# A two-block network on one core: the first head's four slabs projected from raw instead of normalised tokens

## The chip, the cores and the metric

The kernel runs on one core of one Trainium2 chip. The metric is the device time of one execution in microseconds. The kernel before takes 1519.56 us, the median of three runs (1519.48 to 1520.62). A profiled execution, from which every row below comes, is one execution with the hardware profiler on.

The engines are named as the profile names them: PE is TensorE (matmuls), PEld its weight loads, DVE is VectorE, ACT is ScalarE, POOL is GpSimd, and SP is SyncE, which here only issues DMAs.

## The reference

Two blocks over 512 tokens with 1024 features, all in float32. What matters here is how the first block begins: the tokens are normalised, and one wide projection feeds everything else.

```python
def rmsnorm(x, g):
    xf = x.astype(jnp.float32)
    y = xf * lax.rsqrt(jnp.mean(xf * xf, axis=-1, keepdims=True) + EPS)
    return (y * g.astype(jnp.float32)).astype(x.dtype)

h = rmsnorm(x, norm1_g[l])
(hg_q, hg_f, hg_i, hg_g, ml_qk, ml_v, ml_if, ml_o,
 mb_z, mb_xbc, mb_dt, gate_pre) = jnp.split(h @ w_in[l], split_at, axis=-1)
log_f = jnp.log(lb + (1.0 - lb) * jax.nn.sigmoid(hg_f.astype(f32)))
o_hg = hgrn2_scan(jax.nn.silu(hg_q)..., log_f..., hg_i...)     # 8 heads, 128 wide
y_hg = rmsnorm(o_hg, hg_norm_g[l]).reshape(B, S, HG_W) * jax.nn.silu(hg_g)
```

The normalisation is a product per token and a gain per feature: h[t, d] = x[t, d] * g[d] * r[t], with r[t] the reciprocal root mean square of token t. Since r does not depend on d, (h @ W)[t, :] = r[t] * ((x * g) @ W)[t, :]. After the projection come three recurrent branches (HGRN2, mLSTM and Mamba-2), their gated mix, a feed-forward network, and a second block with convolution and windowed attention.

## The kernel before, in words

**Tiles.** Features lie on the 128 partitions and tokens along the free dimension, so a normalised activation is eight feature tiles of 128x512. Weights come as slabs: 128 output columns by 1024 inputs, 512 KB each, 245 of them, through four slots of the tile `raw` in the order in which they are used. Float32 accuracy is reached by splitting each operand in a high half, rounded to the type that PE takes at full pace, and a low half, the rest: `wh` and `wl` of a weight slab (ScalarE rounds `wh`, GpSimd subtracts for `wl`, in two halves at L447), `hh` and `hl` of the normalised tokens, `yh` and `yl` of other activations. `project` issues, for each of the eight feature tiles, three matmuls of 128x512: high times high (L519), high weight times low data (L522), low weight times high data (L523), all into one PSUM bank.

**Order of the work.** Each engine has a program written out by hand, with semaphores between them. PE's program is a row of projections with the branches' small matmuls put between them: the slabs of head u+1 are projected while head u's recurrence is evaluated. Head 0 therefore has only its four slabs F, Q, G, I (numbers 0 to 3) in the prologue, and slab 4 is the first that is projected inside the head loop (`hg_tile(0, ...)`).

**The prologue.** The token rows arrive in four blocks of 128 (`xs`). ScalarE squares and sums each, and makes r for two blocks at a time (L1061, L1065, L1067). DVE multiplies (`xn`, L1708). PE turns the blocks by transposes into six PSUM banks (L549; the last two tiles later, L562), ScalarE reads a bank with the gain into `hh` (L1074), DVE the rest into `hl` (L1715). PE then projects slab 0 tile by tile as the halves appear, with slab 1 interleaved, and slabs 2 and 3. The high halves of slabs 0 to 3 are made by ScalarE, DVE and twice by GpSimd. Two bias matmuls (L555) go in between. Behind the projections, ScalarE and DVE turn head 0's results into its gate and its query (`hg_sigmoid`, `hg_forget`, `hg_first`, L1752 to L1763), and DVE rounds the matrices `onr` and `kbr` (L1771, L1773), for which PE waits before the head loop. Head 0's first sums are L1904 to L1911 on DVE.

**Banks.** Projections alternate between the two banks `acc[0]` and `acc[1]`, which `acc_free0` and `acc_free1` hand back; the others, `b2` to `b7`, belong to the branches.

Of the kernel before, what the change touches and what calls it, by code (L numbers as in the profile page):

```python
# [93 lines left out]
W_LINE = 1024  # L94

# [38 lines left out]
def build(nc, slabs, x, xt, par_d, const_d, onehot_d, bias_scratch, row_scratch, out):  # L134
    with ExitStack() as ctx:
        start = -(-nc.sbuf_base // 64) * 64

        def arena(at):
# [57 lines left out]
        names = """params_in ident_in onr_set masks_in x_in0 x_in1 x_in2 x_in3 onehot_in pre_hi slab_hi slab_split slab_used acc_free0 acc_free1 zero_set  # L196
            pre_h1 xt_in pro_sq pro_rs pro_n pro_tr nrm_rs nrm_h nrm_hi nrm_lo lt_sq lt_add lt_hi lt_lo lt_ss lt_step lb_step
# [9 lines left out]
            at_silu at_sq at_sl kbr_set at_ss at_tr at_rs at_v at_n at_nh at_nl at_s at_l at_mx at_ex at_sum at_p at_pt at_o at_y  # L207
# [198 lines left out]
        def _(sp):  # L406
# [7 lines left out]
            for b in range(NB):  # L414
                sp.dma_start(xs[:, b, :], x.rearrange("a (b p) d -> p (a b) d", p=P)[:, b, :]
                             ).then_inc(S[f"x_in{b}"], 16)
            for j in range(4):
                load(j, j, 0)
                if j == 1:
                    sp.dma_start(oneh[0:64, :], onehot_d[0:64, :]).then_inc(S["onehot_in"], 16)  # L420
# [15 lines left out]
        def _(pool):  # L436
            nc.gpsimd.memset(zero[:, :], 0.0).then_inc(S["zero_set"], 1)
            pool.wait_ge(S["zero_set"], 1)
# [11 lines left out]
            pool.wait_ge(S["pro_n"], NB)  # L450
            pool.wait_ge(S["pre_hi"], 1)
            slab_lo(0)
            pool.wait_ge(S["pre_h1"], 1)
            slab_lo(1)
            for j in (2, 3):
                pool.wait_ge(slab_in[j], 16)
                pool.tensor_tensor(slab(wh, j), slab(raw, j), zero[:, 0:1].broadcast_to([P, KT * P]), ALU.add
                                   ).then_inc(S["pre_hi"], 1)
                pool.wait_ge(S["pre_hi"], j)
                slab_lo(j)  # L460
            def slabs_lo(first, end):
                with pool.Fori(first // 4, end // 4) as it:
                    for i in range(4):
                        pool.wait_ge(S["slab_hi"], it * 4 + (i - 3))
                        slab_lo(i)
# [9 lines left out]
            pool.wait_ge(S["slab_hi"], J_SMALL - 3)  # L475
# [20 lines left out]
            slabs_lo(J_MB0 + 7, N_SLABS)
            for j in range(N_SLABS // 4 * 4, N_SLABS):
                pool.wait_ge(S["slab_hi"], j - 3)
# [4 lines left out]
        def _(pe):  # L503
            mm = pe.matmul

            def project(j0, it=None, k=0, src=(hh, hl), n=KT, base=0, t0=None, first=True, last=True,
                        ready=(), order=(), lo=None, late=None):

                t0 = j0 if t0 is None else t0
                bank, s = acc[t0 % 2], j0 % 4  # L510
                pe.wait_ge(S["slab_split"], lin(2 * (j0 + 1), it, 2 * k) if lo is None else lo)
                if first:
# [31 lines left out]

            pe.wait_ge(S["ident_in"], 16)
            for b in range(NB):
                pe.wait_ge(S["pro_n"], b + 1)
                for f in range(6):
                    ins = pe.transpose(blk(psum[2 + f], b), xn[:, b, f * P:(f + 1) * P], ident)  # L549
                    if b == NB - 1:  # L550
                        ins.then_inc(S["pro_tr"], 1)
            pe.wait_ge(S["params_in"], 16)
            pe.wait_ge(S["onehot_in"], 16)
            for c in range(2):
                mm(acc[1][32 * c:32 * c + AT_HEADS, :], par[0:64, PAR["rel"]:PAR["rel"] + AT_HEADS],  # L555
                   oneh[0:64, c * T:(c + 1) * T], start=True, stop=True).then_inc(S["wb_mm"], 1)

            def turn_in(f):

                pe.wait_ge(S["nrm_lo"], f - 5)  # L560
                for b in range(NB):
                    ins = pe.transpose(blk(psum[2 + f % 6], b), xn[:, b, f * P:(f + 1) * P], ident)  # L562
                ins.then_inc(S["pro_tr"], 1)

            def first(f):

                project(J_HG, order=(f,), first=f == 0, last=f == KT - 1, ready=[(S["nrm_hi"], f + 1)],
                        late=(S["nrm_lo"], f + 1), lo=1 if f < KT // 2 else 2)

            def second(f):  # L570

                project(J_HG + 1, order=(f,), first=f == 0, last=f == KT - 1, lo=3 if f < KT // 2 else 4)
# [55 lines left out]
            def hg_half(s, u, p, j0, it):  # L628
                U = unit[p]
                before = not isinstance(u, int) or u > 0  # L630
                if s == 2:
                    pe.wait_ge(S["hg_ph"], u + 1)
# [405 lines left out]
        def _(act):  # L1038
# [19 lines left out]
            def norm_in():  # L1058
                for b in range(NB):
                    act.wait_ge(S[f"x_in{b}"], 16)  # L1060
                    A(xq[:, b, :], xs[:, b, :], ACT.Square, accum_out=x_ss[:, 0, b:b + 1]).then_inc(S["pro_sq"], 1)  # L1061
                    if b % 2:
                        ss, rs = x_ss[:, 0, b - 1:b + 1], x_ss[:, 1, b - 1:b + 1]
                        act.wait_ge(S["pro_sq"], b + 1)
                        A(rs, ss, ACT.Ln, scale=1.0 / D, bias=EPS).then_inc(S["pro_rs"], 1)  # L1065
                        act.wait_ge(S["pro_rs"], b)
                        A(rs, rs, ACT.Exp, scale=-0.5).then_inc(S["pro_rs"], 1)  # L1067
                act.wait_ge(slab_in[0], 16)
                A(wh[:, 0].rearrange("p k f -> p (k f)"), raw[:, 0].rearrange("p k f -> p (k f)"), ACT.Copy
                  ).then_inc(S["pre_hi"], 1)  # L1070
                act.wait_ge(S["params_in"], 16)
                for f in range(KT):
                    act.wait_ge(S["pro_tr"], f + 1)
                    A(hh[:, f, :], psum[2 + f % 6][:, :], ACT.Identity, scale=pc("norm1", f)  # L1074
                      ).then_inc(S["nrm_hi"], 1)
                    if f == 2:
                        act.wait_ge(S["wb_mm"], 2)
                        for c in range(2):
                            A(wrow[:, c * T:(c + 1) * T], acc[1][32 * c:32 * c + AT_HEADS, :], ACT.Copy
                              ).then_inc(S["wb_ev"], 1)  # L1080
                    if f == 3:
                        act.dma_start(con[:, K_BD:N_CONST], const_d[:, K_BD:]).then_inc(S["masks_in"], 16)
# [1576 lines left out]
```

## Time and profile before

| | us |
|---|---|
| median of three runs | 1519.56 |
| the profiled execution's own time | 1519.61 |
| its span, first to last instruction | 1517.8 |
| PE busy | 1504.9 |
| VectorE busy | 809.9 |
| ScalarE busy | 737.8 |
| GpSimd busy | 665.3 |

The span is what the profile's rows cover; the execution's own time is 1.8 us longer. Times in the rows are counted from the span's start. A matmul of 128x512 is shown with 0.39 us, but one starts every 0.227 us, since they are pipelined: durations of PE overlap, and starts are what counts. The granted clock is the share of full speed that the chip's throttle is recorded to have allowed PE.

### The profile page before, as it was taken

Reading aid. Unit: us, or ns where it says so; the run is one execution under the profiler, and the core shown is the slowest. Engines: PE = TensorE matmul, PEld = TensorE weight load, DVE = VectorE, ACT = ScalarE, POOL = GpSimd, SP = SyncE. Lnnn points to the kernel's source line nnn. Section 1 sums busy time; section 2 is a strip of 40 time slices with the busy share of each in tenths; the row PEclk is TensorE's granted clock in tenths of the full one; section 3 lists DMA queues with packets and bytes.
Section 4 is the critical chain, followed back from the end, with each engine's and each line's share of the span. In section 5 each row is a group of like instructions: output and inputs, shape, how many; then the busy total and the mean of one; then the engine's idle time right before and its main releaser. Section 6 shows DMA issues by size and latency. Waiting matters only on the chain.

```text
span 1517.8 us, 20835 instructions
## 1 busy us (share of the span) xinstructions
PE 1504.9 (99%) x7144; PEld 1231.6 (81%) x7144; DVE 809.9 (53%) x1387; ACT 737.8 (49%) x1177; POOL 665.3 (44%) x510
## 2 busy tenths in 40 slices
PE   7999999999999999999999999999999999999999
PEld 6888888888888888888888888888888887777777
DVE  4677778542347731677633445554542335756761
ACT  6667665424346432466653444444443344545551
POOL 5433433444544454343344444444455554334432
PEclk9999999999999999999999999999999999999999
DMA  5222222333322333223333323333333342222222
GB/s 191 84 70 70 83 70 70 97 97 114 125 84 70 107 116 97 83 100 109 105 110 96 95 96 97 96 97 97 97 99 109 110 140 91 84 94 94 84 58 95
DMA packets 40023, 147.21 MB, mean 97 GB/s; under 512 B 4400, under 2 KB 4912, under 8 KB 38928
## 3 DMA queue, kind: packets, MB, share of 16 engines
q1 hardware_dynamic: 37088, 132.79, 27.4%
q10 hardware_dynamic: 2864, 13.45, 2.3%
q8 instruction: 47, 0.77, 0.2%
q14 instruction: 24, 0.20, 0.0%
HBM read 144.05 MB, written 2.18 MB: 96 GB/s over the span
## 4 chain that ended last, share of the span: by engine, by line
PE 98%; DVE 1%; ACT 0%; DMA 0%; issue 0%; SPq 0%; DVEq 0%
PE bank L519 27%; PE bank L523 27%; PE bank L522 27%; PE bank L736 3%; PE bank L1008 3%; PE bank L623 1%; PE bank L754 1%; PE bank L927 1%; PE bank L917 1%; PE bank L908 1%; PE bank L676 0%; PE bank L999 0%; PE bank L678 0%; DMA xs<-x 0%; PE bank L664 0%; PE bank L549 0%
## 5 line engine op out<-in xcount | busy, mean ns | idle before, releaser
L447 POOL TENSOR_TENSOR wl<-raw,wh 128x512 fp32r<-128x512 f32 x488 | 645.6, 1345 | 831.5 <-ACT wh L1051 819.8
L519 PE MATMUL bank<-hh,wh 128*128 128x512 f32 x832 | 331.6, 399 | 0.1
L523 PE MATMUL bank<-hh,wl 128*128 128x512 f32 x832 | 324.6, 390 | 0.0
L522 PE MATMUL bank<-hl,wh 128*128 128x512 f32 x832 | 324.0, 389 | 0.0
L1051 ACT ACTIVATE wh<-raw 128x1024 fp32r<-128x1024 f32 x241 | 252.8, 1051 | 134.3 <-DMA raw<-slabs 134.2
L519 PE MATMUL bank<-yh,wh 128*128 128x512 f32 x800 | 314.7, 393 | 0.6 <-DVE au L2354 0.4
L523 PE MATMUL bank<-yh,wl 128*128 128x512 f32 x800 | 311.5, 389 | 0.0
L522 PE MATMUL bank<-yl,wh 128*128 128x512 f32 x800 | 311.5, 389 | 0.0
L523 PEld LDWEIGHTS bank<-hh,wl 128*128 128x128 f32 x832 | 156.1, 188 | 33.7
L519 PEld LDWEIGHTS bank<-hh,wh 128*128 128x128 f32 x832 | 156.3, 188 | 33.1 <-issue 2.7
L522 PEld LDWEIGHTS bank<-hl,wh 128*128 128x128 f32 x832 | 156.5, 188 | 30.9
L519 PEld LDWEIGHTS bank<-yh,wh 128*128 128x128 f32 x800 | 150.2, 188 | 36.9 <-issue 6.5
L523 PEld LDWEIGHTS bank<-yh,wl 128*128 128x128 f32 x800 | 150.2, 188 | 31.8
L522 PEld LDWEIGHTS bank<-yl,wh 128*128 128x128 f32 x800 | 150.2, 188 | 30.2
L2297 DVE TENSOR_TENSOR f_t<-bank,rsn 128x512 f32<-128x512 f32 x44 | 30.4, 692 | 110.8 <-PE bank L523 108.4
L519 PE MATMUL bank<-fh,wh 128*128 128x512 f32 x176 | 68.5, 389 | 0.0
L522 PE MATMUL bank<-fl,wh 128*128 128x512 f32 x176 | 68.5, 389 | 0.0
L523 PE MATMUL bank<-fh,wl 128*128 128x512 f32 x176 | 68.5, 389 | 0.0
L2260 DVE TENSOR_TENSOR xT<-xT,bank 128x512 f32<-128x512 f32 x16 | 11.0, 688 | 101.0 <-PE bank L523 101.0
L1863 DVE SCALAR_TENSOR_TENSOR unit<-bank,par,unit 128x511 f32<-128x511 f32 (+2 forms) x72 | 53.9, 749 | 2.6
L1565 ACT ACTIVATE f_g<-f_t,par 128x512 f32<-128x512 f32 x22 | 18.0, 816 | 67.5 <-DVE f_t L2297 67.4
L1686 ACT ACTIVATE a_l<-a_l,a_st 128x512 f32<-128x512 f32 x32 | 23.2, 724 | 45.5 <-DVE a_st L2399 45.4
(356 smaller groups left out, 2021.0 us busy)
## 6 DMA issues: line engine op xcount, KB each, us to landing
raw<-slabs SPq DMA_DIRECT2D x245, 512.0 KB, 3.5
xT<-row_scratch ACTq DMA_DIRECT2D x6, 1024.0 KB, 4.8
xs<-x SPq DMA_DIRECT2D x4, 512.0 KB, 5.8
xT<-xt ACTq DMA_DIRECT2D x2, 1024.0 KB, 7.0
wb<-bias_scratch ACTq DMA_DIRECT2D x1, 1792.0 KB, 8.7
wb<-bias_scratch ACTq DMA_DIRECT2D x2, 896.0 KB, 4.4
out<-a_l SPq DMA_DIRECT2D x4, 256.0 KB, 4.7
out<-au SPq DMA_DIRECT2D x3, 256.0 KB, 2.0
```

The costliest lines, as they stand in the source:

```text
L447: pool.tensor_tensor(slab(wl, i, half), slab(raw, i, half), slab(wh, i, half).bitcast(F32), ALU.subtract).then_inc(S["slab_split"], 1)
L519: mm(bank[:, :], wh[:, s, b, :], xh, start=first and i == 0, stop=False)
L522: mm(bank[:, :], wh[:, s, b, :], xl, start=False, stop=False)
L523: ins = mm(bank[:, :], wl[:, s, b, :], xh, start=False, stop=last and i == len(order) - 1)
L623: ins = mm(dims((b3, b2)[j % 2], a * P // 2, (P, 2), (1, P // 2)), blk(zk[j % 3], a), dims(zq[j % 4], P * a + h, (2 * P - h, 2), (2 * h, n ...
L736: ins = mm(bank[:, :], blk(x_[:, k, :], b), w[u][:, n * T:(n + 1) * T], start=k == 0 and c == 0, stop=k == KT - 1 and c == 2)
L1008: ins = mm(bank[:, :], w[u][:, n * T + b * P:n * T + (b + 1) * P], v[:, k, :], start=i == 0 and n == 0 and c == 0, stop=i == 3 and n == 1 ...
L1051: A(wh[:, i].rearrange("p k f -> p (k f)"), raw[:, i].rearrange("p k f -> p (k f)"), ACT.Copy).then_inc(S["slab_hi"], 1)
L1565: A((f_g, f_v)[v][p][:, :], f_t[v][:, :], ACT.Identity, scale=pc("fcw", lin(3 * NF * v + 3 * p + 2, it, 6)), bias=pc("fcb", lin(p + NF * v ...
L1686: A(a_l[i % 4][:, :], a_l[i % 4][:, :], ACT.Exp, bias=a_st[:, i, 0:1], accum_out=a_st[:, i, 1:2]).then_inc(S["at_ex"], 1)
L1863: ins = STT(dst[:, s:], bank[:, 0:T - s], pc(w, 4 * i + k), dst[:, s:], ALU.mult, ALU.add)
L2297: TT(f_t[v][:, :], acc[j0 % 2][:, :], rsn[:, :], ALU.mult).then_inc(acc_free[j0 % 2], 1)
```

## The change

Slabs 0 to 3 are no longer projected from normalised tokens. SP now loads the transposed raw tokens (`xT`, in three parts) right behind slab 0. ScalarE multiplies by the gain and rounds into `yh`, DVE makes the rest `yl`, and PE projects F, Q, G and I from these, with F and Q in `acc[0]` and `acc[1]`, G in `b6` and I in `b7`. Before them stand 12 matmuls on a zeroed tile. ScalarE makes the high halves of all four slabs.

The token rows are still loaded, behind slabs 1 and 2, for their sums of squares. The factors r are laid on the diagonals of four 128x128 blocks (`rs_diag`) and multiplied by a matrix of ones, which spreads them over all partitions of `b2`; ScalarE copies them to `rs_all`. `raw_out` multiplies each of the four results by `rs_all`. For all later slabs, DVE makes the normalised tiles from `xT`, gain and `b2` in two PSUM banks in turn (`normed`), ScalarE rounds them to `hh` (`normed_hi`), and DVE subtracts for `hl` (`normed_lo`). PE's slab 4 waits for them.

```diff
+            load(0, 0, 0)
+            for i in range(3):
+                features_in(i)
+            load(1, 1, 0)
+            tokens_in(0)
+            load(2, 2, 0)
+            tokens_in(1)
+            load(3, 3, 0)
...
+            pe.wait_ge(S["zero_set"], 2)
+            for _ in range(WARM):
+                mm(blk(b5, 0), spare[:, :], spare[:, :], start=True, stop=True)
+
+            for f in range(KT):
+                project(J_HG + HG_F, src=(yh, yl), order=(f,), first=f == 0, last=f == KT - 1,
+                        ready=[(S["raw_hi"], f + 1)], late=(S["raw_lo"], f + 1), lo=1 if f < KT // 2 else 2)
+            project(J_HG + HG_Q, src=(yh, yl))
+            project(J_HG + HG_G, src=(yh, yl), order=range(2), last=False, own=b6)
             pe.wait_ge(S["ident_in"], 16)
             for b in range(NB):
...
+                pe.wait_ge(S["pro_d"], b + 1)
+                ins = mm(blk(b2, b), ones, rs_diag[:, b, :], start=True, stop=True)
+            ins.then_inc(S["pro_b"], 1)
+            project(J_HG + HG_G, src=(yh, yl), order=range(2, KT), first=False, own=b6)
+            project(J_HG + HG_I, src=(yh, yl), own=b7)
...
-            first(0)
-            first(1)
-            turn_in(6)
-            first(2)
-            turn_in(7)
-            pe.wait_ge(S["wb_ev"], 2)
-            for f in range(3, KT):
-                second(f - 3)
-                first(f)
-            for f in range(KT - 3, KT):
-                second(f)
-            for i in range(2, 4):
-                project(J_HG + i)
             pe.wait_ge(S["masks_in"], 16)
-            pe.wait_ge(S["onr_set"], 1)
-            pe.wait_ge(S["kbr_set"], 1)
+            pe.wait_ge(S["ones_set"], 2)
...
-                    project(j, it, 8)
+                    project(j, it, 8, ready=[(S["nrm_lo"], f + 1) for f in range(KT)] if it is None and u == 0 else ())
...
+            def raw_out(i, bank, done):
+
+                dve.wait_ge(S["slab_used"], i + 1)
+                if i == HG_G:
+                    TT(unit[0][:, i, :], bank[:, :], rs_all[:, :], ALU.mult).then_inc(done, 1)
+                    return
+                (a, b), (p, q), (c, d) = even_odd(bank[:, :]), even_odd(rs_all[:, :]), slots(unit[0][:, i, :])
+                TT(c, a, p, ALU.mult)
+                TT(d, b, q, ALU.mult).then_inc(done, 1)
+
+            def normed(f):
+
+                wait(dve, S["nrm_lo"], f - 1)
+                STT((b3, b4)[f % 2][:, :], xT[:, f, :], pc("norm1", f), b2[:, :], ALU.mult, ALU.mult).then_inc(S["nrm_t"], 1)
+
+            def normed_lo(f):
+
+                dve.wait_ge(S["nrm_hi"], f + 1)
+                TT(hl[:, f, :], (b3, b4)[f % 2][:, :], hh[:, f, :].bitcast(F32), ALU.subtract).then_inc(S["nrm_lo"], 1)
```

On ScalarE, this is the start of the program before, from the table load to the first high halves (`xq` squares, `x_ss` factors):

```order
L1045 ACT_TABLE_LOAD
L1061 ACTIVATE xq,x_ss<-xs 128x1024 [waits x_in0]
L1061 ACTIVATE xq,x_ss<-xs 128x1024 [waits x_in1]
L1065 ACTIVATE x_ss<-x_ss 128x2 [waits pro_sq]
L1067 ACTIVATE x_ss<-x_ss 128x2 [waits pro_rs]
...
L1069 ACTIVATE wh<-raw 128x1024 [waits slab_in0]
L1074 ACTIVATE hh<-bank,par 128x512 [waits pro_tr,params_in]
```

And the same place now, where `wh<-raw` is a slab's high half and `yh<-xT` a raw feature tile's:

```order
L1047 ACTIVATE wh<-raw 128x1024 [waits slab_in0]
L1072 ACTIVATE yh<-xT,par 128x512 [waits f_in0,params_in]
L1072 ACTIVATE yh<-xT,par 128x512 [waits f_in0]
L1072 ACTIVATE yh<-xT,par 128x512 [waits f_in1] x2
L1072 ACTIVATE yh<-xT,par 128x512 [waits f_in2] x4
L1047 ACTIVATE wh<-raw 128x1024 [waits slab_in1]
L1075 ACTIVATE small<-small 128x8 [waits lb_step]
L1053 ACTIVATE xq,x_ss<-xs 128x1024 [waits x_in0] x2
```

The squares moved behind the eight feature tiles and slab 1's high half; slab 1's high half, before on DVE, stands behind all eight feature tiles.

On DVE, this is the end of the prologue before, from head 0's gate to its first sum:

```order
L1752 TENSOR_SCALAR hg_88<-hg_86,small 128x512 [waits hg_f,lb_step]
L1761 TENSOR_SCALAR hg_90<-hg_88 128x512 [waits hg_k]
L1763 TENSOR_TENSOR hgq_95<-unit_62,hg_88 128x512 [waits hg_silu]
L1768 COPY hga_93<-pair 128x512
L1768 COPY hga_94<-pair 128x512
L1771 CAST onr<-con 128x128 [waits ident_in,lb_step]
L1773 CAST kbr<-con 128x128 [waits masks_in]
L1774 TENSOR_TENSOR small<-par 128x8
L1904 TENSOR_TENSOR hgp<-unit_62,hg_90 128x512 [waits hg_z]
```

And now its last part (L1786 is `normed`, L1791 `normed_lo`, L1780 and L1781 `raw_out` of I):

```order
L1786 SCALAR_TENSOR_TENSOR bank<-xT,par,bank 128x512 [waits nrm_lo]
L1791 TENSOR_TENSOR hl<-bank,hh 128x512 [waits nrm_hi]
L1769 TENSOR_SCALAR hg_91<-hg_89 128x512 [waits hg_k]
L1771 TENSOR_TENSOR hgq_96<-unit_62,hg_89 128x512 [waits hg_silu]
L1786 SCALAR_TENSOR_TENSOR bank<-xT,par,bank 128x512 [waits nrm_lo]
L1791 TENSOR_TENSOR hl<-bank,hh 128x512 [waits nrm_hi] x2
L1780 TENSOR_TENSOR unit_62<-bank,rs_all 128x256 [waits slab_used]
L1781 TENSOR_TENSOR unit_62<-bank,rs_all 128x256
L1820 CAST kbr<-con 128x128 [waits masks_in]
L1821 TENSOR_TENSOR small<-par 128x8
L1951 TENSOR_TENSOR hgp<-unit_62,hg_91 128x512 [waits hg_z]
```

Sixteen instructions on the normalised tiles now stand between the copied factors and `kbr`, in between head 0's own.

On PE, the step into slab 4 before:

```order
L519 MATMUL bank<-hh,wh 128x512
L522 MATMUL bank<-hl,wh 128x512
L523 MATMUL bank<-hh,wl 128x512
L519 MATMUL bank<-hh,wh 128x512 [waits slab_split,kbr_set,acc_free0,onr_set,masks_in]
L522 MATMUL bank<-hl,wh 128x512
```

And now, after slab I and the two bias matmuls (`oneh`):

```order
L529 MATMUL bank<-yh,wl 128x512
L570 MATMUL bank<-oneh,par 8x512 [waits onehot_in,params_in]
L570 MATMUL bank<-oneh,par 8x512
L525 MATMUL bank<-hh,wh 128x512 [waits acc_free0,slab_split,nrm_lo,ones_set,masks_in]
L528 MATMUL bank<-hl,wh 128x512
L529 MATMUL bank<-hh,wl 128x512
L525 MATMUL bank<-hh,wh 128x512 [waits nrm_lo]
```

The bias matmuls moved here, and each tile of slab 4 waits for its low half; `ones_set` reaches 2 with `kbr`.

## Rows read from the trace of the kernel before

**Rows 1.** The page: span and busy time of two engines.
```profile
span 1517.8 us, 20835 instructions
...
PE 1504.9 (99%) x7144; PEld 1231.6 (81%) x7144; DVE 809.9 (53%) x1387; ACT 737.8 (49%) x1177; POOL 665.3 (44%) x510
```

**Rows 2.** Waits of PE, whole span: total us, times, longest.
```profile
PE bank L549 <- DVE xn L1708: 9.1, 1, 9.1
PE bank L917 <- DVE a_l L2407: 0.6, 2, 0.3
```

**Rows 3.** Chain of waits, in order of time: start us, us, what.
```profile
1.19 5.36 DMA xs<-x
...
9.12 5.14 PE bank L549 x24
14.26 0.96 PE bank L555 x4
```

**Rows 4.** Timeline of PE: start us, us, engine, line, operation.
```profile
37.96 0.39 PE L519 MATMUL bank<-hh,wh 128*128 128x512 f32 x1
...
43.40 0.62 PE L623 MATMUL bank<-hgq,hgk 128*128 128x128 f32 x4
```

**Rows 5.** Stretches: busy us of each engine, granted clock, DMA share, GB/s.
```profile
0.00:9.80 9.80, 0.68 (x4) 0.71 (x5) 1.42 (x2) 5.60 (x10) 0.30 (x5) 1.00 0.81 308
...
37.95:1517.80 1479.85, 1476.07 (x7013) 1207.81 (x7011) 792.20 (x1356) 713.69 (x1138) 644.72 (x491) 1.00 0.29 95
```

**Rows 6.** Timeline of ACT in the prologue.
```profile
4.71 1.06 ACT L1061 ACTIVATE xq<-xs 128x1024 f32<-128x1024 f32 x1 [1.75 <-DMA xs<-x]
...
17.11 2.43 ACT L1074 ACTIVATE hh<-bank,par 128x512 fp32r<-128x512 f32 x4
...
30.07 1.28 ACT L1042 ACT_TABLE_LOAD   x1
```

**Rows 7.** Timeline of POOL in the prologue.
```profile
19.64 2.54 POOL L447 TENSOR_TENSOR wl<-raw,wh 128x512 fp32r<-128x512 f32 x2
...
30.13 2.54 POOL L447 TENSOR_TENSOR wl<-raw,wh 128x512 fp32r<-128x512 f32 x2 [3.48 <-ACT wh L1051]
34.34 6.08 POOL L447 TENSOR_TENSOR wl<-raw,wh 128x512 fp32r<-128x512 f32 x4 [1.67 <-ACT wh L1051]
```

**Rows 8.** Timeline of DVE in the prologue.
```profile
17.24 3.38 DVE L1715 SCALAR_TENSOR_TENSOR hl<-bank,par,hh 128x512 fp32r<-128x512 f32 x5 [0.86 <-ACT hh L1074]
...
25.31 0.42 DVE L1723 TENSOR_SCALAR unit<-bank 128x256 f32<-128x256 f32 x1 [4.35 <-PE bank L523]
25.65 0.41 DVE L1724 TENSOR_SCALAR unit<-bank 128x256 f32<-128x256 f32 x1
...
28.17 0.55 DVE L1752 TENSOR_SCALAR hg<-hg,small 128x512 f32<-128x512 f32 x1 [1.09 <-ACT hg L1169]
28.75 0.43 DVE L1761 TENSOR_SCALAR hg<-hg 128x512 f32<-128x512 f32 x1
32.03 1.19 DVE L1763 TENSOR_TENSOR hgq<-unit,hg 128x512 f32<-128x512 f32 x1 [2.85 <-ACT unit L1153]
...
33.92 0.23 DVE L1771 CAST onr<-con 128x128 fp32r<-128x128 f32 x1
...
34.28 0.68 DVE L1904 TENSOR_TENSOR hgp<-unit,hg 128x512 f32<-128x512 f32 x1
34.88 1.51 DVE L1905 TENSOR_TENSOR hgp<-hgq,hg 128x256 f32<-128x256 f32 x1
...
41.72 0.95 DVE L1911 TENSOR_TENSOR hgpl<-hgp,hgph 128x768 fp32r<-128x768 f32 x1
```

**Rows 9.** Instructions that touch the tile con: duration ns min/median/max, starts, forms.
```profile
L549 PEld LDWEIGHTS bank<-con,xn x24: 178/230/230, 9.1 to 13.8; 128*128 128x128 f32 x24
...
L562 PEld LDWEIGHTS bank<-con,xn x8: 138/140/143, 16.4 to 18.0; 128*128 128x128 f32 x8
```

More of the change, by code:

```diff
@@ L94 @@
 W_LINE = 1024
+WARM = 12
 def ml_slab(u, i):
@@ L448, in slab_lo @@
                                        ).then_inc(S["slab_split"], 1)
[L450 to L459, printed above, removed]
+            for j in range(4):
+                pool.wait_ge(S["slab_hi"], j + 1)
                 slab_lo(j)
@@ L506, in project @@
             def project(j0, it=None, k=0, src=(hh, hl), n=KT, base=0, t0=None, first=True, last=True,
-                        ready=(), order=(), lo=None, late=None):
+                        ready=(), order=(), lo=None, late=None, own=None):
                 t0 = j0 if t0 is None else t0
-                bank, s = acc[t0 % 2], j0 % 4
+                bank, s = acc[t0 % 2] if own is None else own, j0 % 4
                 pe.wait_ge(S["slab_split"], lin(2 * (j0 + 1), it, 2 * k) if lo is None else lo)
-                if first:
+                if first and own is None:
                     wait(pe, acc_free[t0 % 2], lin(t0 // 2, it, k // 2))
@@ L554, in _ @@
             for c in range(2):
[L555 removed]
+                mm(b5[32 * c:32 * c + AT_HEADS, :], par[0:64, PAR["rel"]:PAR["rel"] + AT_HEADS],
                    oneh[0:64, c * T:(c + 1) * T], start=True, stop=True).then_inc(S["wb_mm"], 1)
[L558 to L572, printed above, removed]
[L574 to L586 removed]
             pe.wait_ge(S["masks_in"], 16)
[L588 to L589 removed]
+            pe.wait_ge(S["ones_set"], 2)
             def sum_all(bank, h, l, sem):
@@ L1056, in _, with first_hi @@
             exp_tables()
[L1058 to L1070, printed above, removed]
+            def first_hi(j):
+                act.wait_ge(slab_in[j], 16)
+                A(wh[:, j].rearrange("p k f -> p (k f)"), raw[:, j].rearrange("p k f -> p (k f)"), ACT.Copy
+                  ).then_inc(S["slab_hi"], 1)
@@ L1076, in norm_in @@
[L1076 to L1082, printed above, removed]
-                        act.wait_ge(S["wb_ev"], 2)
-                        act.dma_start(bias_scratch, wrow[:, :]).then_inc(S["wb_out"], 16)
+                    act.wait_ge(S[f"f_in{min(f // 2, 2)}"], 16)
@@ L1735, in _, with clamp_f @@
             dve.wait_ge(S["lb_step"], 6)
+            dve.wait_ge(S["ident_in"], 16)
+            dve.tensor_copy(onr[:, :], ones).then_inc(S["ones_set"], 1)
+            for b in range(NB):
+                dve.wait_ge(S["pro_rs"], b // 2 * 4 + 4)
+                TS(rs_diag[:, b, :], ident, x_ss[:, 1, b:b + 1], None, ALU.mult).then_inc(S["pro_d"], 1)
+            for i in range(2):
+                dve.tensor_copy(at2[i][:, :], zero[:, 0:1].broadcast_to([P, T])).then_inc(S["lb_step"], 1)
+            def clamp_f(j0, dst, it=None):
+                dve.wait_ge(S["slab_used"], lin(j0 + 1, it, 8))
+                (a, b), (c, d) = even_odd(acc[j0 % 2][:, :]), slots(dst)
+                TS(c, a, -40.0, None, ALU.max)
+                TS(d, b, -40.0, None, ALU.max).then_inc(acc_free[j0 % 2], 1)
             step = [0]
```

146 lines of the change are left out of this document (92 added, 54 removed).

## The prediction

> **What bounds the kernel now.** I read the page first. TensorE (PE) is busy for 1504.9 of 1517.8 us, VectorE (DVE), the next, for about half [rows 1]. PE's waits come next: 9.1 us in one piece at the start, and the next largest group is 0.6 us in two [rows 2]. So the program is a wait of 9.1 us, a prologue, and then a dense stream of matmuls. The chain of waits shows what the 9.1 us are: the token rows' DMA (and, between its rows, ScalarE's squares), then PE's transposes [rows 3]. The timeline of PE gives the boundary I work with: the first matmul of slab 4 (the first slab of head 1) issues at 37.96 us, the next block's first at 43.40 [rows 4]. A slab is therefore 5.44 us: 24 matmuls at 0.227, or 0.68 per feature tile. What follows 37.96 has 1476 busy us in 1480 [rows 5] and is not touched. The change is worth the shift of that boundary, called S, plus any stall that it leaves behind. The profiled execution took 1519.61 us, 1.8 more than its span and 0.05 above the median of the three timed runs (1519.56); I add the shift to 1519.61.
>
> **The change: what PE could gain.** Removed from PE are the 24 + 8 transposes and the wait for the normalised tokens. Added are 12 matmuls on zeros, four small matmuls of the factors and a wait before slab 4. The new front end needs slab 0, the constants and parameters, the feature tiles and slab 1, in SP's new order. At the rate of before, 308 GB/s over the first 9.8 us, 3.02 MB are in by then [rows 5]. Slab 0, constants and parameters are 0.92 MB and all features 2.10 more, so the last features land at 9.8, with 0.3 us to the semaphore 10.1; slab 1 (3.54 MB) follows at 11.8 at the latest.
> ScalarE starts slab 0's high half when it has landed, at 4.7 like the first token block [rows 6], and it lasts 1.0 to 1.06; POOL's two halves take 2.54 [rows 7], so they end at 7.1 and 8.4. DVE's first low feature tile has two inputs in SBUF and, I take it, waits behind POOL until 8.4, done at 9.1. The other seven follow at 0.68, so the F slab ends at about 14.4. Then PE stands: ScalarE makes slab 1's high half only after its eighth feature tile. Four tiles at 0.60 (four took 2.43 [rows 6]) after 10.1 is 12.5; the copy of slab 1 ends at 13.5; POOL's 2.54 ends at 16.05, with the semaphores 16.2. Slab Q starts at 16.2.
> From there PE issues Q (5.44), two tiles of G (1.36), four factor matmuls (eight records, 0.75; four such take 0.62 with their tail [rows 4]), the rest of G (4.08) and I (5.44), and the bias matmuls (0.96 [rows 3]). It would be ready for slab 4 at 34.2 us, 3.7 earlier than before. The zero matmuls end by about 6 us, before any operand is there, and cost nothing.
>
> **The new wait.** Slab 4 now needs all of hh and hl, and the rounded mask block (kbr), which is the last of DVE's new list. All of that list starts after the factors are spread over a bank and copied: 16.2 + 5.44 + 1.36 + 0.75 + 0.2 for the tail + 0.6 for ScalarE's copy + 0.1 = 24.65 us. From there DVE issues, all in a row:
> eight products xT*gain*factor at 0.67 = 5.36 (five of the same form took 3.38, that is 0.67 from one start to the next [rows 8]); eight subtractions at 0.60 = 4.80 (a TENSOR_TENSOR of 128x512 starts at 34.28, the next instruction at 34.88 [rows 8]); six half-bank products for F, Q and I at 0.34 = 2.04 (25.31 to 25.65), and G 0.60; clamp 0.42, forget 0.55, kk 0.33, zq 0.60, kbr 0.23 [rows 8]. The sum is 14.93, to 39.6.
> Three things lengthen it. The last subtraction needs ScalarE's eighth copy, which stands behind silu(G) and a table load of 1.28 [rows 6]; walking both lists by these durations ScalarE is 0.9 late there. Four products wait for the subtraction issued just before them instead of overlapping it, 0.3 in all. The product zq meets POOL's slab 5: the same instruction took 1.19 at 32.03 with POOL in its slab, and a like one 0.68 at 34.28 before POOL began [rows 7, 8], so 0.5. Slab 4 starts at 41.3 instead of 37.96: +3.35 us. PE idles from 34.2 to 41.3, 7.1 us.
> Bounds: without contention and with the first 0.3 saved, 39.6 (+1.6); with each of the 16 long instructions a full 0.74, half of those beside POOL's two slabs held to 1.5, and slab Q at 16.7, about 44 (+6). I take 3.35 because every term is the nearest row.
> How much DVE suffers from POOL is where a rule of the Trainium skill can be weighed. The rows: beside POOL's 34.34 to 40.42, the instruction of 256 columns with two SBUF inputs at 34.88 took 1.51, while the five with a PSUM input at 17.24, the last two of them beside POOL's 19.64, kept 0.67 [rows 7, 8]. The Trainium skill, SBUF — State Buffer, section "Who interferes with whom", says that a VectorE instruction with two SBUF inputs blocks against GpSimd and one with at most one does not; by that rule, which the trace agrees with, the 16 new instructions, each with a PSUM input, are free of it. Were the trace otherwise, and each such instruction 0.85 longer, as the 34.88 row is against the 0.67, the five or six that lie beside slabs 4 and 5 would add some 4 us, and S would be 45.
>
> **The clock.** The granted clock column shows 1.00 in every stretch [rows 5], but the instructions tell otherwise. After 9.1 idle us 24 transposes take 5.14 us, 0.214 each [rows 3], and their weight loads 230 ns in the median; eight later ones of the same shape load in 140 ns [rows 9]. I read that as the lower of the two levels (1.2 GHz) from 9.1 to about 13.8, 4.7 us, and 2.4 GHz after. After 7.1 idle us I expect the same: 4.7 us of slab 4 at half the clock, in which half the work is done, a loss of 2.35. Bounds: 0 (the fall does not come) and 4.7; by the pace of the transposes alone (0.214 against 0.14) it would be 1.6.
> The Trainium skill, TensorE: Matmul & The Clock Gate, section "What's actually happening", likewise has an idle array at 1.2 GHz by default and back at 2.4 after sustained work, which speaks against a change that opens a gap in a dense stream.
>
> **Who comes late afterwards.** Head 0's remaining sums need DVE from the first gate product (34.28) to hgpl's end (42.67), 8.4 us; PE asks for them about 8.55 us after S (slab 4's 5.44, two small products, four tiles of slab 5 at 0.68) [rows 8]. Now DVE starts them at S, so 0.15 us remain, and POOL has two halves there instead of four. ScalarE is about as late. I charge 0; if it shows, 1 us.
>
> **Sum.** +3.35 + 2.35 = +5.7: 1525.3 us.
>
> **Rivals.**
> B, the same wait, no clock fall. For it: the granted clock row never leaves 1.00 [rows 5]. Against: the slow transposes. 1519.6 + 3.35 = 1523.0.
> C, faster: DVE keeps up, PE alone sets the prologue and slab 4 starts at 34.2, -3.7: 1515.9. It decides when DVE's list after 24.65 takes 9.5 us or less. For it: two-input work is the costly part, and single-input instructions of 512 columns take 0.43 (28.75 [rows 8]); if all 16 took that, the list would still be 11.7. Against: every 512-column row with two inputs is at 0.67 or above.
> D, slower still: the front gap is felt too. After the zero matmuls end near 6 us, PE has one matmul until 9.1; if the F slab then runs wholly at the half pace (24 at 0.43 = 10.3) it ends at 19.4, Q starts 3.2 later, and everything behind with it: 1528.5. If the pace recovers in 4.7 us as before, only 0.6.
> E, the change does what it says but the features come later than the old rate allows: part of D in effect.
>
> **Chances.** Forecast 0.60, B 0.22, C 0.05, D with E 0.13. About 0.2% (3.0 us) is what a measurement of this kernel can tell from no change, so "same" is 1516.5 to 1522.6: it takes somewhat under half of B, whose spread of 1.5 us reaches there, and a little of C. Faster 0.04, same 0.11, slower 0.85. The range 1521.6 to 1529.0 takes in B, most of the forecast's bounds, and D.
>
> **What would show it.** Right: PE idle before slab 4's first matmul for 5 to 9 us, released by DVE (kbr or the last subtraction); a PE idle of 1 to 3 us between F and Q, released by POOL; slab 4's weight loads slow at its start; the body unchanged. Wrong: slab 4 starting before 38 us (C); no slow matmuls behind the gap (B); F's matmuls 0.43 apart (D); PE waits beyond 45 us, which I hold to be nothing.

## Result, and the profile after

| | before | after |
|---|---|---|
| time, median (lowest to highest; runs) | 1519.89 us (1519.48 to 1520.62; 5) | 1526.43 us (1525.80 to 1526.58; 5) |
| profiled execution: time, span | 1519.61, 1517.8 | 1526.43, 1524.0 |

The five runs of before are the three of the forecast and two more. The ratio is 1.0041, with a 95% interval of 1.003 to 1.0052: slower by more than the 0.2% that can be told. The forecast was 1525.3 us, the range 1521.6 to 1529.0. In the table and in every comparison below a single execution is only read for its profile; times are medians.

The page of after, against [rows 1]: PE is busy 5.3 us more with as many instructions as before, so some of them take longer.
```profile
span 1524.0 us, 20912 instructions
...
PE 1510.2 (99%) x7144; PEld 1234.9 (81%) x7144; DVE 824.3 (54%) x1408; ACT 743.5 (49%) x1184; POOL 659.3 (43%) x509
```
PE's waits, against [rows 2] (total us, times, longest). The 9.1 us at the start have become several short ones, and one of 6.3 us that the mask block kbr, the last of DVE's list, ends. It was to be 7.1.
```profile
PE bank L525 <- DVE kbr L1820: 6.3, 1, 6.3
PE bank L525 <- ACT yh L1072: 1.5, 1, 1.5
PE bank L553 <- POOL spare_row L452: 1.0, 1, 1.0
PE bank L528 <- DVE yl L1719: 0.8, 1, 0.8
...
PE bank L525 <- POOL wl L461: 0.3, 1, 0.3
```
PE's timeline, against [rows 4]. The F slab starts at 7.78, Q at 16.48, slab 4 at 41.25 (before: 37.96), and the block behind it at 49.39 (before: 43.40). Slab 4 therefore takes 8.14 us and not 5.44. Behind its first matmul (0.77) the line at 41.81 is the first of eleven that take 0.63 and start 0.43 apart; from 46.87 they start about 0.23 apart. Head 0's first sums come at 52.61.
```profile
7.78 0.47 PE L525 MATMUL bank<-yh,wh 128*128 128x512 f32 x1 [1.53 <-ACT yh L1072]
...
16.48 0.50 PE L525 MATMUL bank<-yh,wh 128*128 128x512 f32 x1 [0.30 <-POOL wl L461]
...
33.93 1.03 PE L570 MATMUL bank<-oneh,par 64*8 64x512 f32 x4
41.25 0.77 PE L525 MATMUL bank<-hh,wh 128*128 128x512 f32 x1 [6.29 <-DVE kbr L1820]
41.81 0.63 PE L528 MATMUL bank<-hl,wh 128*128 128x512 f32 x1
...
49.39 0.62 PE L607 MATMUL bank<-hgq,hgk 128*128 128x128 f32 x4
...
52.61 0.39 PE L622 MATMUL bank<-hgph,onr 128*128 128x512 f32 x1
```
Stretches of after (columns as in [rows 5]). The granted clock is about half (0.53) for nine matmuls of F and again (0.50) in the first part of slab 4, and full in between.
```profile
9.04:12.48 3.44, 3.44 (x9) 2.66 (x9) 3.36 (x6) 2.61 (x5) 0.00 (x0) 0.53 1.00 410
...
16.48:34.90 18.42, 18.42 (x84) 14.43 (x84) 11.64 (x26) 12.69 (x22) 7.32 (x6) 1.00 0.55 189
...
41.25:46.51 5.26, 5.26 (x13) 4.10 (x14) 5.13 (x8) 4.63 (x9) 3.79 (x3) 0.50 0.05 9
...
49.39:1524.00 1474.61, 1470.77 (x6989) 1203.37 (x6987) 790.63 (x1350) 709.23 (x1129) 637.42 (x487) 1.00 0.30 95
```
The same last stretch of before:
```profile
43.40:1517.80 1474.40, 1470.62 (x6989) 1203.31 (x6987) 787.61 (x1350) 709.82 (x1129) 641.64 (x489) 1.00 0.29 95
```
So the span's 6.2 us are 3.29 (41.25 less 37.96), 2.70 (8.14 less 5.44) and 0.21 (1474.61 less 1474.40).

DVE's timeline of after, against [rows 8]: the first product, the product zq, the last subtraction, kbr, one of head 0's instructions of 256 columns, and the rounding remainder hgpl.
```profile
25.13 0.76 DVE L1786 SCALAR_TENSOR_TENSOR bank<-xT,par,bank 128x512 f32<-128x512 f32 x1 [3.51 <-ACT rs_all L1084]
...
36.78 0.68 DVE L1771 TENSOR_TENSOR hgq<-unit,hg 128x512 f32<-128x512 f32 x1
...
39.66 0.69 DVE L1791 TENSOR_TENSOR hl<-bank,hh 128x512 fp32r<-128x512 f32 x1 [0.93 <-ACT hh L1064]
...
40.93 0.22 DVE L1820 CAST kbr<-con 128x128 fp32r<-128x128 f32 x1
...
42.75 1.52 DVE L1944 TENSOR_TENSOR hg<-hg 128x256 f32<-128x256 f32 x1
...
47.25 2.04 DVE L1958 TENSOR_TENSOR hgpl<-hgp,hgph 128x768 fp32r<-128x768 f32 x1
```
ACT's timeline, against [rows 6]: the last four raw feature tiles, the factors' copy, and the table load that makes the last copy of hh late.
```profile
10.30 2.56 ACT L1072 ACTIVATE yh<-xT,par 128x512 fp32r<-128x512 f32 x4 [0.83 <-DMA xT<-xt]
...
24.50 0.60 ACT L1084 ACTIVATE rs_all<-bank 128x512 f32<-128x512 f32 x1 [2.81 <-PE bank L563]
...
37.74 1.28 ACT L1031 ACT_TABLE_LOAD   x1
39.03 0.60 ACT L1064 ACTIVATE hh<-bank 128x512 fp32r<-128x512 f32 x1
```
POOL's timeline, against [rows 7]: the low halves of slabs 1, 5 and 6, two instructions each.
```profile
13.89 2.54 POOL L461 TENSOR_TENSOR wl<-raw,wh 128x512 fp32r<-128x512 f32 x2 [5.45 <-ACT wh L1047]
...
36.79 3.02 POOL L461 TENSOR_TENSOR wl<-raw,wh 128x512 fp32r<-128x512 f32 x2 [1.61 <-ACT wh L1037]
42.46 2.96 POOL L461 TENSOR_TENSOR wl<-raw,wh 128x512 fp32r<-128x512 f32 x2 [2.65 <-ACT wh L1037]
```

### The profile page after: what moved, and what is told of

Same layout as the page of the kernel before. It is cut to its first block, busy times and chain, and to the rows that moved or that the text cites. A ratio compares the mean times of both kernels' runs of the same rounds, so it can differ in the third digit from the quotient of the medians.

```text
span 1524.0 us, 20912 instructions
## 1 busy us (share of the span) xinstructions
PE 1510.2 (99%) x7144; PEld 1234.9 (81%) x7144; DVE 824.3 (54%) x1408; ACT 743.5 (49%) x1184; POOL 659.3 (43%) x509
## 4 chain that ended last, share of the span: by engine, by line
PE 96%; DVE 1%; ACT 1%; DMA 1%; issue 0%; POOL 0%; SPq 0%; DVEq 0%
PE bank L525 27%; PE bank L529 26%; PE bank L528 26%; PE bank L722 3%; PE bank L994 3%; PE bank L607 1%; PE bank L740 1%; PE bank L913 1%; PE bank L903 1%; PE bank L894 1%; DMA xT<-xt 1%; PE bank L662 0%; PE bank L985 0%; PE bank L664 0%; PE bank L650 0%
## 5 line engine op out<-in xcount | busy, mean ns | idle before, releaser
L525 PE MATMUL bank<-yh,wh 128*128 128x512 f32 x832 | 328.1, 394 | 2.4 <-ACT yh L1072 1.5
L525 PE MATMUL bank<-hh,wh 128*128 128x512 f32 x800 | 320.2, 400 | 6.3 <-DVE kbr L1820 6.3
L528 PE MATMUL bank<-yl,wh 128*128 128x512 f32 x832 | 324.7, 390 | 0.8 <-DVE yl L1719 0.8
L529 PE MATMUL bank<-yh,wl 128*128 128x512 f32 x832 | 324.8, 390 | 0.0
L529 PE MATMUL bank<-hh,wl 128*128 128x512 f32 x800 | 313.1, 391 | 0.0
L528 PE MATMUL bank<-hl,wh 128*128 128x512 f32 x800 | 312.5, 391 | 0.0
L525 PEld LDWEIGHTS bank<-yh,wh 128*128 128x128 f32 x832 | 156.6, 188 | 40.9 <-issue 6.5
L529 PEld LDWEIGHTS bank<-yh,wl 128*128 128x128 f32 x832 | 156.5, 188 | 33.2
L528 PEld LDWEIGHTS bank<-yl,wh 128*128 128x128 f32 x832 | 156.6, 188 | 32.4 <-DVE yl L1719 1.1
L529 PEld LDWEIGHTS bank<-hh,wl 128*128 128x128 f32 x800 | 150.7, 188 | 32.6
```

The lines of the kernel that those rows point to most:

```text
L525: mm(bank[:, :], wh[:, s, b, :], xh, start=first and i == 0, stop=False)
L528: mm(bank[:, :], wh[:, s, b, :], xl, start=False, stop=False)
L529: ins = mm(bank[:, :], wl[:, s, b, :], xh, start=False, stop=last and i == len(order) - 1)
```

## The experiments

Theory A is the prediction's: a wait for DVE's list, then matmuls at the lower clock. Its rivals were that the clock is not what the slow matmuls cost, that only the place of the mask block holds PE up, and that something later is dearer. The diffs are against the changed kernel, but for the last run, which is against the kernel before. Each ratio is to runs of the kernel before on the same chip, whose median was 1520.23 us for fill, kbr_early, two_products and no_warm, 1520.06 for fill_half, reordered, reordered_slab1 and before_warm, and 1519.66 for acts_alone and acts_and_kbr. Where a run is compared with after by the medians, the two can be from different chips.

**The gap filled with matmuls on zeros (fill).**
```
             pe.wait_ge(S["masks_in"], 16)      # ahead of this line:
+            pe.wait_ge(acc_free[1], 1)
+            for _ in range(28):
+                mm(blk(acc[1], 0), spare[:, :], spare[:, :], start=True, stop=True)
```


> 28 zero matmuls (of the kind at the start) stand in PE's gap between the bias matmuls and slab 4, on acc[1], which is free there. Nothing else changes. My theory (the gap costs twice: 3.3 us because slab 4 waits for DVE's list, and 2.7 us because PE comes back at the lower clock): slab 4 still starts at 41.2 to 41.4, takes 5.5 instead of 8.1 us, and the time falls by 2.3 to 2.7 us, to about 1523.9. Rival (slab 4 is slow for another reason, such as operands or weights that come late or DVE, ACT and POOL working beside it): it stays at 8.1 us and the time at 1526.4.


1523.6 us, ratio 1.002 [1.0011, 1.0029]. Its PE timeline: the zero matmuls (56 records) run up to slab 4's first, whose successor starts 0.30 behind it and not 0.56 as in after; the block behind slab 4 starts at 47.07, 5.56 us after slab 4's first, and head 0's first sums at 50.29.
```profile
35.14 6.52 PE L574 MATMUL bank<-spare_row 128*128 128x128 f32 x56
41.51 0.47 PE L525 MATMUL bank<-hh,wh 128*128 128x512 f32 x1
41.81 0.39 PE L528 MATMUL bank<-hl,wh 128*128 128x512 f32 x1
...
47.07 0.62 PE L610 MATMUL bank<-hgq,hgk 128*128 128x128 f32 x4
...
50.29 0.39 PE L625 MATMUL bank<-hgph,onr 128*128 128x512 f32 x1
```
Slab 4 starts as late as in after (41.51 against 41.25), and the clock's part is gone. Slab 4 is 2.6 us shorter (8.14 less 5.56), the time 2.8 by the medians. The clock term is shown.

**Half the filling (fill_half).** As above with `range(14)`.

> As fill, with 14 zero matmuls instead of 28: the gap before slab 4 is then about 3.2 us of idle time behind 3.1 us of zero matmuls. If a gap of this length costs the clock as the whole one does, slab 4 takes 8 us and the time is that of the changed kernel, 1526.4; if it does not, slab 4 takes 5.6 us and the time is that of fill, 1523.6. I expect the latter with 0.5.


1525.49 us, ratio 1.0036 [1.0022, 1.005], which is that of after within the intervals. PE's timeline shows 3.0 idle us in place of 6.3, and slab 4 slow all the same: the next block starts 8.4 us after it.
```profile
35.25 3.39 PE L574 MATMUL bank<-spare_row 128*128 128x128 f32 x28
41.62 0.77 PE L525 MATMUL bank<-hh,wh 128*128 128x512 f32 x1 [2.98 <-issue]
```
In this execution a wait of half the length gives nothing of the clock back. It is the longest of the five (1526.86); the other four took 0.75 to 1.9 us less and have no rows here, so whether each of them lost as much is open.

**The mask block rounded early (kbr_early).**
```
             TS(unit[0][:, HG_F, :], unit[0][:, HG_F, :], -40.0, None, ALU.max).then_inc(acc_free[0], 1)
+            dve.wait_ge(S["masks_in"], 16)
+            dve.tensor_copy(kbr[:, :], cc(K_BD)).then_inc(S["ones_set"], 1)
...
-            dve.wait_ge(S["masks_in"], 16)
-            dve.tensor_copy(kbr[:, :], cc(K_BD)).then_inc(S["ones_set"], 1)
```


> The rounding of kbr moves on DVE from the end of the list to behind head 0's clamp (26.9 us). PE's wait before slab 4 is then met early, and each tile of slab 4 waits for its own low half only. Theory A (the whole DVE list is the cost, wherever PE waits for it): slab 4 starts near 35.3 and ends near 41.1 instead of 49.4, but PE then waits for head 0's own DVE work, which starts at 41.1 as before: first small product of head 0 at about 44, first sums at about 49 instead of 52.6; time 1522 to 1523. Rival B (the place of kbr alone is the cost, DVE has room behind it): no wait behind slab 4, and the time falls by 8 us, to about 1518. Rival C (the subtractions gate it, kbr does not): slab 4 starts at 40.3, time 1525.5.


1523.44 us, ratio 1.0021 [1.0012, 1.003]. PE's timeline has three waits where after has one, 5.0 us together:
```profile
35.57 0.47 PE L525 MATMUL bank<-hh,wh 128*128 128x512 f32 x1 [0.55 <-DVE hl L1791]
...
43.89 0.70 PE L607 MATMUL bank<-hgq,hgk 128*128 128x128 f32 x4 [2.34 <-ACT hgk L1136]
...
49.45 0.47 PE L622 MATMUL bank<-hgph,onr 128*128 128x512 f32 x1 [2.12 <-DVE hgpl L1958]
```
Slab 4 starts 5.7 us earlier, but the time falls by 3.0, to 0.4 above the range that theory A gave: DVE's work for head 0 is now the late one, and the last of the three waits brings the lower clock (from 49.45 to the next block at 55.02 it is 5.57 us, where the same matmuls take 3.90 in fill, 50.29 to 54.19). The rival, the mask block's place alone, fell. Its place matters, since it kept each feature tile of slab 4 from starting when that tile was ready, but behind it stands the length of the list. The profiled execution, 1524.30, was the longest of the eleven.

**Six of the eight products left out (two_products).**
```
+                if f > 1:
+                    return
                 wait(dve, S["nrm_lo"], f - 1)   # in normed(f)
```


> Leaves out six of the eight products xT*gain*factor on DVE: feature tiles 2 to 7 of hh and hl are taken from the two banks that hold tiles 0 and 1. DVE's list is 6 x 0.67 = 4.0 us shorter, nothing else. Theory (slab 4 starts when DVE's list is done): slab 4 starts 3 to 4 us earlier, at 37.3 to 38.3; the gap falls from 6.3 to about 3 us, and if that still costs the clock the time is about 1522.8, if not about 1520.2. Rival (DMA, POOL or ScalarE hold slab 4): the start stays at 41.2 and the time at 1526.4.


1524.2 us, ratio 1.0029 [1.0018, 1.0041], 2.2 below after by the medians, which the intervals don't separate. Slab 4 started at 40.37, 0.9 earlier, where 3 to 4 were expected: a miss. DVE's timeline of this run says why:
```profile
34.93 0.69 DVE L1794 TENSOR_TENSOR hl<-bank,hh 128x512 fp32r<-128x512 f32 x1 [1.73 <-ACT hh L1065]
...
38.78 0.69 DVE L1794 TENSOR_TENSOR hl<-bank,hh 128x512 fp32r<-128x512 f32 x1 [1.63 <-ACT hh L1065]
```
With 4.0 us of work fewer DVE stands and waits for ScalarE, whose copies of hh take no product as their signal any more but the subtraction two tiles back (not in the lines above). That cost ScalarE one wait of 0.33 us, at 30.43; from there to 38.76, the end of its last copy, it does not pause. ScalarE's list (the copies of hh, slabs 4 and 5, three activations, two table loads of 1.28 us) is about as long as DVE's, and that was not in the prediction but for its 0.9 us at the end. So it takes work off both engines to start slab 4 earlier. The full clock also came back sooner here, after 3.1 us of slow matmuls (from 40.37) and not 5.3: slab 4 took 7.05 us and not 8.14. With the 0.9 at its start that makes the 2.0 by which this profiled span (1522.0) is shorter than after's.

**No zero matmuls at the start (no_warm).** `WARM = 0` in place of 12.

> Without the 12 zero matmuls at the start. Theory (slab Q starts when POOL has slab 1's low half, 16.5 us, and the F slab ended 0.3 us before that): F starts at the same 7.8 us; its slow pace may last 1 to 2 us longer, so that Q starts 0 to 1 us later; time 1526.4 to 1527.4. Rival (the zero matmuls are what brings the clock up in the middle of F): F runs wholly at the slow pace, 10.3 us from 9.0, Q starts 3 us later, time 1529.4.


1525.53 us, ratio 1.0034 [1.0022, 1.0047]: the same as after within the intervals, and 0.9 below the range that was expected, a miss. PE's timeline of this run:
```profile
7.83 0.77 PE L525 MATMUL bank<-yh,wh 128*128 128x512 f32 x1 [7.83 <-ACT yh L1072]
...
13.98 0.58 PE L525 MATMUL bank<-yh,wh 128*128 128x512 f32 x1
14.39 0.39 PE L528 MATMUL bank<-yl,wh 128*128 128x512 f32 x1
```
F is slow up to 14.39 where after's was slow up to 12.48, and Q follows it without a gap, where after had stood 0.3 us for POOL. Warming PE up cannot gain more than that here, since Q needs slab 1's low half. Without it slab 4 starts at 41.57, 0.3 later. Its slow stretch is shorter (3.5 us, not 5.3), so that the block behind it comes at 48.78, before after's 49.39.

**Three moves at once (reordered).** The mask block early, as above. The factor matmuls right behind slab Q. And on ScalarE, for head 0 only:
```
-                exp_tables()                    # behind silu(G)
+                if it is not None or j0 != J_HG or u != 0:
+                    exp_tables()
...
                     hg_round(u)
+                    if it is None and not before:
+                        slab_hi(J_HG + HG_I + 3)
...
                     hg_keep(2, u)
+                    if not before:
+                        exp_tables()
...
-            slab_hi(J_HG + HG_I + 3)
```


> Four moves in the changed kernel, no work added or removed but one: kbr is rounded behind head 0's clamp; the four factor matmuls come right behind slab Q instead of two tiles later (DVE's and ScalarE's lists start 1.4 us earlier); ScalarE loads the exponential tables in front of head 1's sigmoid instead of in front of its eighth normalised tile (the last subtraction 0.9 us earlier); and ScalarE makes slab 6's high half behind head 0's first sums instead of in front of them (POOL is then idle beside DVE's two-input instructions, which took 1.0 us more each in four or five cases, 4 us). Theory (the lists of DVE and ScalarE up to head 0's first sums are the cost, PE's own work is not): DVE starts head 0's first gate product at about 38.9 instead of 41.1 and ends hgpl at about 44.5 instead of 49.3; PE reaches head 0's first small product at 40.5 to 41.5 and its sums at about 44.5, against 43.4 and 46.5 in the kernel before; time 1517 to 1518. Rival (the raw projection cannot win, since the DVE work that it adds comes back wherever it is put): 1520 or more.


1518.12 us, ratio 0.9989 [0.998, 0.9998], 0.1 above the expected range (its four moves are these three, with ScalarE's two counted apart). It beats the changed kernel by 8.3 us by the medians and the kernel before by 1.9, the latter under the 0.2% but with an interval that leaves 1 out. PE waits 0.6 us before head 0's block at 41.47 and nowhere later in the prologue. DVE's timeline: the instruction that took 1.52 in after (42.75), and hgpl.
```profile
40.77 0.42 DVE L1947 TENSOR_TENSOR hg<-hg 128x256 f32<-128x256 f32 x1
...
42.41 0.96 DVE L1961 TENSOR_TENSOR hgpl<-hgp,hgph 128x768 fp32r<-128x768 f32 x1
```
GpSimd starts slab 6 at 43.40 here, behind these instructions. In after it ran beside them. The slow instructions are moved, not gone: three later ones, at 44.92, 46.34 and 47.86, now take 1.50, 1.31 and 1.24 us beside GpSimd, but PE doesn't wait for them.

**The same with slab 1 loaded and rounded earlier (reordered_slab1).** Slab 1's transfer and its high half stand between the first four feature tiles and the last four, and the factor matmuls behind G's first tile.

> As reordered, and slab 1 is loaded and rounded between the fourth and the fifth feature tile, the factor matmuls stand behind G's first tile. Theory (PE waits at slab Q for POOL, and the lists of DVE and ScalarE set the end of the prologue): slab Q starts at about 15 instead of 16.5, the bias matmuls end 1.5 us earlier, but the factors come from tokens that land at the same time, so the lists start only 0.7 us earlier than in reordered, and so the time is 0.5 to 0.9 us below that of reordered. Rival (PE's own work is what sets the end): 1.5 us below it.


1518.86 us, ratio 0.9992 [0.9983, 1.0001]: no better, a miss. Slab Q does follow F without waiting, but F itself now waits 0.3 us for a low half, and the factor matmuls start at 22.89, later than in reordered (22.30). With the later factors DVE's list starts later and PE waits 1.2 us for head 0's keys where it waited 0.6.

**ScalarE's order alone, and with the mask block (acts_alone, acts_and_kbr).** The parts of the diff of reordered that their names say; the factor matmuls stay in slab G.

> The changed kernel with ScalarE's order alone (table load and slab 6's high half moved behind head 0's rounding); mask block and factor matmuls as in the changed kernel. Theory (PE stands before slab 4 for the mask block whatever ScalarE does, and the clock is lost in that gap; all that gets shorter is the lateness of the last subtraction): slab 4 starts at 40.3 to 41.0, takes 8.1 us, 1525.4 (1524.8 to 1526.0), within 1.5 us of the changed kernel. Rival (ScalarE's order alone gives the gain seen with it): below 1522.

> The changed kernel with two of the three moves of the run 'reordered': the mask block rounded early (DVE), and ScalarE's order (the table load and slab 6's high half behind head 0's rounding). The factor matmuls stay inside slab G. Theory (each move takes its own wait away, and the ScalarE order frees DVE's head 0 products from GpSimd's slab 6): slab 4 starts at 35.1 to 35.6, PE then waits 1.3 to 1.7 us on the gate keys of head 0 (0.6 in 'reordered', the factors come 0.9 later), the gate products at 42 take 0.42 and not 1.5, no second wait on hgpl; about 1518.9 (1518.5 to 1519.4), so 4.5 us below the run with the mask block alone (1523.4). Rival (the factor matmuls' place is what made 'reordered' fast, since everything of DVE hangs on it): 1521.5 or more.

acts_alone: 1524.93 us, ratio 1.0033 [1.0021, 1.0045]; 1.5 us below after, which the intervals don't separate. PE's largest wait:
```profile
PE bank L525 <- DVE kbr L1824: 5.4, 1, 5.4
```
acts_and_kbr: 1519.48 us, ratio 1.0 [0.9991, 1.0009], 0.1 above the expected range. PE's largest wait in slab 4's stretch:
```profile
PE bank L607 <- ACT hgk L1136: 1.4, 1, 1.4
```
Alone the two moves give 1.5 and 3.0 us, together 7.0, by the medians (of runs on different chips, but the medians of the kernel before are within 0.6 of each other), of which the 1.5 is not told from nothing. The spans of the executions scatter less, and their medians give 0.8, 2.4 and 6.3 (1523.9 for after; 1523.1, 1521.5 and 1517.6). Why they are worth more together is read from the rows. ScalarE's order spares DVE four slow instructions (1.52, 1.30, 1.38 and 2.04 us in after against 0.42, 0.43, 0.28 and 0.96 in acts_and_kbr). While slab 4 waits for the mask block nobody needs that time: in acts_alone hgpl is ready at 45.0 and asked for at 51.7. Once slab 4 starts at 35.6, head 0's products are what PE waits for, and each of these microseconds counts. The factor matmuls' move gives about 1 more: the profiled spans are 1517.3 without it and 1516.3 with it, and PE's wait for the keys 1.4 and 0.6.

**The kernel before, with zero matmuls ahead of its transposes (before_warm).**
```
+            pe.wait_ge(S["zero_set"], 2)
+            for _ in range(22):
+                mm(blk(b7, 0), spare[:, :], spare[:, :], start=True, stop=True)
```


> The kernel before with 22 zero matmuls in front of its transposes (PE is idle there for 9.1 us). Theory (the transposes ran at the lower clock from 9.1 to 13.8): with PE at work from 1.0 us on they run at 0.14 to 0.15 us each, the last six end 0.8 to 1.0 us earlier, and the time falls by as much, to 1518.7. Rival (as in the changed kernel, where the first matmuls behind the zero ones were still slow): no change, or up to 0.5 us slower if the zero matmuls last beyond 9.1 us.


1518.56 us, ratio 0.9991 [0.9982, 1.0]. PE's timeline:
```profile
1.03 7.10 PE L548 MATMUL bank<-spare_row 128*128 128x128 f32 x44 [1.03 <-POOL spare_row L438]
8.95 1.50 PE L553 MATMUL bank<-con,xn 128*128 128x128 f32 x12 [0.82 <-DVE xn L1712]
...
42.21 0.62 PE L627 MATMUL bank<-hgq,hgk 128*128 128x128 f32 x4
```
Twelve transposes take 1.50 us, 0.125 each, where [rows 3] has 0.214. The boundary of 43.40 comes at 42.21. So the transposes of before were slow because of the clock, as the prediction read them, and about 1.2 us of that can be had back, where 0.8 to 1.0 were expected; not all of it, since the second twelve now wait 1.00 us for their tokens.

## Why the prediction was right

*S, the start of slab 4:* 41.25 against 41.3. Its parts were near, with two misses that cancel, and that the total fell within 0.05 is luck. The list began 0.48 late (25.13 against 24.65), since Q started at 16.48 and not at 16.2 and the factors' tail and copy took a little longer. The zq product was charged 0.5 for POOL and paid nothing: it started at 36.78, and POOL's half at 36.79. POOL's two halves took 3.02 there, and 2.5 in the slabs before (2.54 at 13.89). The Trainium skill, SBUF — State Buffer, section "Who interferes with whom", says that the order of issue decides which of the two blocks; these two rows agree. The list from 25.13 to 41.15 is 16.0 us: the 14.93 that were added up, ScalarE's lateness of 0.93 as predicted, and 0.16 where 0.8 had been charged (0.3 for products that wait, 0.5 for POOL).

*That the eight feature tiles are needed at once:* imprecise. Slab 4 takes the tiles one after another. It is the mask block, in front of the slab and last on DVE, that made it wait for the whole list. kbr_early starts the slab at 35.57 with its last tiles not made yet. That does not change the sum, because the mask block ended the list in this kernel.

*The clock:* 2.70 against 2.35 with bounds of 0 and 4.7. That it falls in the gap, and what that costs, is shown by fill. The slow stretch lasted 5.26 us (41.25 to 46.51), where the transposes of before suggested 4.7. One number for it is too precise: in the other kernels that had the gap it was 3.1 to 5.7 us, so the term is 1.6 to 2.9 (slab 4's time less 5.44, in two_products and in fill_half).

*The start:* PE was ready for slab 4 at 34.96, 0.8 later than 34.2. F ended at about 16.05, not 14.4, since nine of its matmuls ran at half the clock (9.04 to 12.48). That is rival D in part, and it cost nothing: PE stood 0.30 us for slab 1's low half, which POOL ended at 16.43. Q's own lateness of 0.28 is ScalarE's: its last four feature tiles started at 10.30 and took 2.56, where 10.1 and 2.40 were reckoned, and slab 1's high half stands behind them (the 0.2 of their start is all that rival E came to). The other 0.5 us of PE's lateness lie in Q and behind it and cost little, because PE then idled 6.3 us. The sentence that the zero matmuls cost nothing held, and no gain from them can be told either (no_warm).

*What comes late afterwards:* 0 was charged and 0.21 measured. PE does not wait for hgpl: it ends at 49.29, 8.15 us after DVE began on head 0 at 41.14 (8.4 were reckoned), and PE asks at 52.61. The slow clock is 2.7 us of that room, but the charge of 0 did not need it: in fill, where the clock does not fall, hgpl ends at 49.58 and PE asks at 50.29 without a wait, 0.7 us to spare where 0.15 were reckoned.
```profile
47.53 2.05 DVE L1961 TENSOR_TENSOR hgpl<-hgp,hgph 128x768 fp32r<-128x768 f32 x1
```
The 0.21 lie behind these sums: from the block's start to the next block it is 3.90 us in after (49.39 to 53.29) as before (43.40 to 47.30).

*Rivals:* B (1523.0) fell to the rows of slab 4; a kernel made to fit it, fill, gave 1523.6. C (1515.9) needed a list of 9.5 us, and it was 16.0. 

The sum was 5.7 and the span's 6.2; the profiled execution's time rose by 6.8, of which 0.6 lies outside the span. That part varies from one execution to the next, 1.8 to 2.8 us among the five of after, and isn't explained.

## What to carry to other kernels

Moving an engine's work behind a late input (here 15 us of DVE instructions behind the token factors) costs PE the list's length where PE waits for the list's end, however early PE itself starts; the same work in another order (reordered) cost nothing against the kernel before. Look at what stands last in the list and in front of the next slab: one cast of 0.22 us held a slab whose first tiles had long been ready. And price a gap in PE as the gap plus the clock, and the moves that close it together, not one by one: two moves of 1.5 and 3.0 us by the medians were worth 7.0 at once.

## What the runs showed of the hardware that was not expected

A gap of 3.0 us before slab 4 cost, in the profiled execution of fill_half, as much clock as one of 6.3, and one of 1.4 before head 0's block (acts_and_kbr) none. In kbr_early the matmuls behind the 2.34 us ran at full pace (granted clock 1.00 from 43.89 to 47.33), those behind the 2.12 us that followed after 3.4 busy us did not (0.55 from 49.45 to 53.13).

The pace came back at different times behind gaps of the same kind: after 5.3 us (after), 5.7 (fill_half), 4.4 (acts_alone), 3.5 (no_warm) and 3.1 (two_products) of slab 4. What decides between them no run here tells.

Twelve zero matmuls (24 records) from 1.03 to 6.24 us ran at half pace (0.42 a record in the median, overlapping) but for the last two (0.39 for both together, from 5.86). The F slab's first matmul, behind 1.53 idle us, still took 0.47 as at full pace (0.77 in no_warm); behind the next wait, of 0.79 us, nine were slow (9.04 to 12.48). With 22 zero matmuls, up to 8.13 us, the transposes ran at full pace behind waits of 0.82 and 1.00 us.

The granted clock column is not to be trusted in the first slow stretch of a trace. In no_warm, PE's first matmuls are 0.43 apart and the column reads 1.00 (us, PE, PEld, DVE, ACT, POOL, clock, DMA share, GB/s), where after's reads 0.53 at the same pace:
```profile
9.10:14.20 5.10, 5.08 (x12) 4.03 (x13) 4.82 (x8) 4.09 (x8) 0.26 (x1) 1.00 1.02 418
```
The kernel before shows the same at its transposes, and so does after at its zero matmuls (1.00 from 1.03 to 6.24). There the pace, not the column, told the clock.
